# Compact chunks put together with the other order of the first pair, own cross attention banks for odd heads, and 512-column matmuls in the MLP output halves

## The reference

```python
for l in range(DEPTH):
    h = rmsnorm(x, norm_mix[l])
    if l % 2 == 0:
        qkv, z, b_raw, a_raw, lx, lg = split_cols(h @ hyb_in_w[e], HYB_SIZES)
        mix = concat([gdn_mixer(...), rglru_mixer(...)]) @ hyb_out_w[e]
    else:
        mix = swa_mixer(h @ swa_in_w[o], ...) @ swa_out_w[o]
    x = x + mix
    x = x + cross_attn(rmsnorm(x, norm_cross[l]), rmsnorm(mem, norm_mem[l]), ...)
    x = x + conv_ffn(rmsnorm(x, norm_ffn[l]), ...)

def cross_attn(h, mem_n, wq, wkv, wo, q_norm, k_norm):      # 4 heads of 128
    q = rmsnorm((h @ wq).reshape(bsz, s, X_HEADS, X_HD), q_norm)
    k, v = split_cols(mem_n @ wkv, (X_INNER, X_INNER))
    p = softmax(einsum(q, rmsnorm(k, k_norm)) * X_HD ** -0.5)
    return einsum(p, v) @ wo

def conv_ffn(h, w_in, conv_w, conv_b, w_out):
    gt, up = split_cols(h @ w_in, (D_FF, D_FF))
    gt = causal_dwconv(gt, conv_w) + conv_b
    return (silu(gt) * up) @ w_out
```

## Time and profile before

| | |
|---|---|
| median of 3 runs | 2650.51 us (2649.71 to 2658.74) |
| profiled execution | 2661.51 us, its span 2659.7 us |
| PE busy | 2578.9 us, 97% of the span |
| DVE, ACT busy | 1740.7 us (65%), 1138.4 us (43%) |
| mean granted PE clock | 0.991 of full speed |
| weights read | 800 pieces of 512 KB, 162 GB/s over the span |

### The profile page before, as it was taken

How to read it: one execution, slowest core, us unless ns; L and a number is a source line. 1 busy time by engine, 2 the same in 40 slices (tenths; PEclk the granted TensorE clock), 3 DMA queues, 4 the chain that set the end, 5 groups by cost and what they waited for, 6 DMA issues and landing times.

```text
span 2659.7 us, 47742 instructions
## 1 busy us (share of the span) xinstructions
PE 2578.9 (97%) x18995; PEld 2382.9 (90%) x18995; DVE 1740.7 (65%) x2469; ACT 1138.4 (43%) x1501; POOL 50.2 (2%) x58
## 2 busy tenths in 40 slices
PE   7999999998999999999999999999999999999999
PEld 6889888998988899889989888898888998899889
DVE  6566666666777756775577667766777557764773
ACT  5444443443444434443344445444444334443443
POOL 2000000000000000000000100000000000000000
PEclk9999999999999999999999999999999999999999
DMA  6434444355456565656555543354465655665554
GB/s 201 121 112 131 117 120 135 124 180 165 143 166 189 184 187 175 183 189 192 184 184 182 154 146 109 104 161 141 127 189 184 187 173 185 189 193 183 185 185 149
DMA packets 428452, 432.56 MB, mean 163 GB/s; under 512 B 13802, under 2 KB 425747, under 8 KB 428304
## 3 DMA queue, kind: packets, MB, share of 16 engines
q1 hardware_dynamic: 423776, 422.46, 51.7%
q0 software_dynamic: 2304, 5.85, 0.7%
q10 hardware_dynamic: 2224, 2.11, 0.2%
HBM read 428.27 MB, written 2.10 MB: 162 GB/s over the span
## 4 chain that ended last, share of the span: by engine, by line
PE 86%; DVE 7%; ACT 4%; issue 2%; DMA 1%; POOL 0%; POOLq 0%; SPq 0%; ACTq 0%; DVEq 0%
PE stream L1655 25%; PE stream L1640 14%; PE stream L1641 13%; PE stream L1642 13%; PE stream L1656 13%; ACT scores L920 1%; DVE w_lo L986 1%; PE bank L1624 1%; PE bank L1758 1%; ACT w_hi L550 1%; DMA stage<-in_mem 1%; PE bank L1687 0%; DVE v_buf L1040 0%; DVE k_buf L1040 0%; DVE lru_x L1040 0%
## 5 line engine op out<-in xcount | busy, mean ns | idle before, releaser
L986 DVE TENSOR_TENSOR w_lo<-w_raw,w_hi 128x1024 fp32r<-128x1024 f32 x800 | 964.4, 1222 | 553.0 <-ACT w_hi L550 550.0
L550 ACT CAST w_hi<-w_raw 128x1024 fp32r<-128x1024 f32 x800 | 836.3, 1048 | 827.2 <-PE stream L1642 474.4
L1655 PE MATMUL stream<-h,w_hi 128*128 128x512 f32 x2816 | 995.6, 399 | 0.0
L1656 PE MATMUL stream<-h,w_lo 128*128 128x256 f32 x2816 | 790.9, 281 | 0.0
L1655 PEld LDWEIGHTS stream<-h,w_hi 128*128 128x128 f32 x2816 | 529.2, 188 | 131.8
L1640 PE MATMUL stream<-act,w_hi 128*128 128x256 f32 x2016 | 575.4, 285 | 1.0 <-DVE act L1013 1.0
L1642 PE MATMUL stream<-act,w_lo 128*128 128x256 f32 x2016 | 571.4, 283 | 0.0
L1641 PE MATMUL stream<-act,w_hi 128*128 128x256 f32 x2016 | 571.4, 283 | 0.0
L1656 PEld LDWEIGHTS stream<-h,w_lo 128*128 128x128 f32 x2816 | 532.0, 189 | 0.1
L1640 PE MATMUL stream<-h,w_hi 128*128 128x256 f32 x1536 | 460.2, 300 | 5.3 <-DVE w_lo L986 5.3
L1641 PE MATMUL stream<-h,w_hi 128*128 128x256 f32 x1536 | 438.7, 286 | 0.0
(11 more groups left out here) (397 smaller groups left out, 1612.3 us busy)
## 6 DMA issues: line engine op xcount, KB each, us to landing
w_raw<-in_ffn_in_w SPq DMA_DIRECT2D x352, 512.0 KB, 4.5
w_raw<-in_ffn_out_w SPq DMA_DIRECT2D x176, 512.0 KB, 4.6
w_raw<-in_hyb_in_w SPq DMA_DIRECT2D x96, 512.0 KB, 3.8
w_raw<-in_swa_in_w SPq DMA_DIRECT2D x48, 512.0 KB, 3.6
w_raw<-in_xkv_w SPq DMA_DIRECT2D x32, 512.0 KB, 3.4
w_raw<-in_hyb_out_w SPq DMA_DIRECT2D x32, 512.0 KB, 4.2
w_raw<-in_swa_out_w SPq DMA_DIRECT2D x32, 512.0 KB, 3.5
w_raw<-in_xq_w SPq DMA_DIRECT2D x16, 512.0 KB, 4.0
```

The source lines that it names most:

```text
L550: nc.scalar.copy(whi[:, k], raw[:, n % NRAW]).then_inc(hi_split, 1)
L986: v.tensor_tensor(wlo[:, k], raw[:, n % NRAW], whi[:, k].bitcast(F32), ALU.subtract).then_inc(lo_split, 1)
L1655: mm(bank[:, m, :], whi[:, k, kk, w], h[:, kt, :, :], start=(q == 0 and kk == 0), stop=False, skip_group_check=True)
L1656: last = mm(bank[:, m, 0:TOK], wlo[:, k, kk, w], h[:, kt, 0, :], start=False, stop=(q == 3 and kk == len(kts) - 1), skip_group_check=True)
```

## The change

Four edits in one.

1. The output halves of the MLP call `wide_piece` with `act_` as the source instead of `piece`: per pair of blocks one matmul of 512 columns and one of 256, in place of three of 256. DVE's residual of these groups is now two additions, right halves first, then left halves.
2. In cross attention of layer 1, `turn` and `pv` of the odd heads have banks of their own (`B[3]` and `B[0]`), head 1 is turned and copied right behind head 0, and the first two pieces of the product with `xo_w` are cut in two (`xo_heads`): heads 0 and 1 as soon as they are out, heads 2 and 3 at the end. DVE's `norm(2)` stands ahead of `outp(1)`.
3. Ahead of pair 0, x is turned into four banks instead of two; ACT's rounding of a weight piece stands ahead of the x work of its quarter from quarter 1 on; POOL's parameter DMAs wait for the second quarter of x.
4. In pair 0, DVE copies `ba` at the head of tick 3 instead of its end, and the polynomial chain and what follows it (`gates` 6, 7, 8) stand at ticks 8, 9, 10.

```diff
@@ x_bank, x_turned, x_pv
+        def x_bank(g):
+            return B[(1, 2, 4, 5)[g % 4]]
+        def x_turned(layer, h):
+            return B[3] if layer and h % 2 else B[4]
+        def x_pv(layer, h):
+            return B[0 if layer and h % 2 else 5][:, 0:TOK]
@@ gpsimd
+            pool.wait_ge(x_loaded[1], 16)
             pool.dma_start(wba[:], ...)
@@ scalar
             for q in range(4):
+                if q:
+                    split(q)
                 x_hi(2 * q)
                 x_hi(2 * q + 1)
-                split(q)
+                if q == 0:
+                    split(q)
...
-                if t == 7:
+                if t == 9:
                     tables(LN_EXP)
                     act.wait_ge(cols_in, 1)
...
                     if layer and t == 7:
                         copy(0)
+                        copy(1)
...
                     scale(1)
-                    copy(1)
                     exps(2)
                     exps(3)
@@ vector
-                if t == 3:
-                    dve.wait_ge(ba_done, 1)
-                    v.tensor_copy(ba_rows, B[5][0:16, 0:TOK]).then_inc(ba_copied, 1)
...
-                if t == 6:
+                if t == 8:
                     dve.wait_ge(ln_out, 3)
...
                     if p == 0 and t == 3:
+                        dve.wait_ge(ba_done, 1)
+                        v.tensor_copy(ba_rows, B[5][0:16, 0:TOK]).then_inc(ba_copied, 1)
                         dve.wait_ge(ss_done, 1)
...
-                        residual(g0 + g, g, n + g * q + q - 1, "norm_mix" if norm else None, KT, wide(g0 + g)[:, 1, :])
+                        dve.wait_ge(pieces_done, n + g * q + q)
+                        x2, both = xT[:, 2 * g:2 * g + 2, :], wide(g0 + g)
+                        link(v.tensor_tensor(x2, both[:, :, TOK:512], x2, ALU.add))
+                        v.tensor_tensor(x2, both[:, :, 0:TOK], x2, ALU.add).then_inc(group_evac, 1)
+                        if norm:
+                            dve.wait_ge(group_evac, g0 + g + 1)
+                            split_h(g, x2.rearrange("p k c -> p (k c)"), "norm_mix", KT)
...
                     outp(0)
+                    norm(2)
                     outp(1)
-                    norm(2)
                     norm(3)
@@ tensor
-                    if q:
-                        pe.wait_ge(xt_copied, g - 1)
+                    if q >= 2:
+                        pe.wait_ge(xt_copied, g - 3)
...
-                if t == 7:
+                if t == 9:
                     pe.wait_ge(g_ready, 1)
...
+            def xo_heads(g, heads):
+                n, gi = XO[1] + g, GROUP[XO[1]] + g
+                k = n % NSPLIT
+                pe.wait_ge(xo_out, 4 + heads[-1] + 1)
+                if heads[0] == 0:
+                    pe.wait_ge(lo_split, n + 1)
+                    pe.wait_ge(group_evac, gi - 1)
+                for m in range(2):
+                    for kt in heads:
+                        o = ST[gi % 2][:, m * TOK:m * TOK + TOK]
...
+                if heads[-1] == 3:
+                    last.then_inc(pieces_done, 1)
...
                     if layer and t == 7:
                         turn(0)
+                        turn(1)
...
                     scores(3)
-                    turn(1)
                     pv(0)
                     pv(1)
                     turn(2)
+                    turn(3)
+                    xo_heads(0, (0, 1))
                     pv(2)
-                    turn(3)
+                    xo_heads(1, (0, 1))
                     pv(3)
-                pe.wait_ge(xo_out, 4 * layer + 4)
                 for g in range(8):
-                    piece(XO[layer] + g, GROUP[XO[layer]] + g, 0, 0, act_, range(4))
+                    if layer and g < 2:
+                        xo_heads(g, (2, 3))
+                    else:
...
-                            piece(n + g * q_ + q, g0 + g, q, q_ - 1, act_, range(4 * q, 4 * q + 4), wide(g0 + g)[:, 1, :])
+                            wide_piece(n + g * q_ + q, g0 + g, q, range(4 * q, 4 * q + 4), 0, act_, q_ - 1)
```

More of the change, by code:

```diff
@@ L788, in copy @@
                         act.wait_ge(xo_done, 4 * layer + h - 1)
-                    nc.scalar.copy(xpT[:, h % 2], B[4][:]).then_inc(xpt_copied, 1)
+                    nc.scalar.copy(xpT[:, h % 2], x_turned(layer, h)[:]).then_inc(xpt_copied, 1)
                 def scale(j):
@@ L1353, in outp @@
                     dve.wait_ge(xo_done, 4 * layer + h + 1)
-                    split_act(h, B[5][:, 0:TOK], xo_out)
+                    split_act(h, x_pv(layer, h), xo_out)
                 def scale(j):
@@ L1944, in turn @@
                     pe.wait_ge(xpn, 4 * layer + h + 1)
-                    if h:
-                        pe.wait_ge(xpt_copied, 4 * layer + h)
+                    if layer and h >= 2:
+                        pe.wait_ge(xpt_copied, 4 * layer + h - 1)
+                    elif h and not layer:
+                        pe.wait_ge(xpt_copied, h)
                     for u in range(2):
                         for m in range(2):
-                            last = transpose(B[4][:, m * TOK + u * P:m * TOK + u * P + P],
+                            last = transpose(x_turned(layer, h)[:, m * TOK + u * P:m * TOK + u * P + P],
                                              xp[:, h % 2, u * TOK + m * P:u * TOK + m * P + P])
@@ L1954, in pv @@
                     pe.wait_ge(xpt_copied, 4 * layer + h + 1)
-                    if h:
-                        pe.wait_ge(xo_out, 4 * layer + h)
+                    if layer and h == 1:
+                        pe.wait_ge(n_out, N_XQ[layer] + 2)
+                    elif layer and h >= 2:
+                        pe.wait_ge(xo_out, 4 * layer + h - 1)
+                    elif h:
+                        pe.wait_ge(xo_out, h)
                     for m in range(2):
-                        last = mm(B[5][:, 0:TOK], xv[layer][:, m, h, :], xpT[:, h % 2, m * TOK:m * TOK + TOK],
+                        last = mm(x_pv(layer, h), xv[layer][:, m, h, :], xpT[:, h % 2, m * TOK:m * TOK + TOK],
                                   start=(m == 0), stop=(m == 1))
@@ L1975, in cross @@
                 return scores, turn, pv, sums
+            def xo_heads(g, heads):
[8 more added lines that the diff above has]
+                        o = ST[gi % 2][:, m * TOK:m * TOK + TOK]
+                        w = slice(m * P, m * P + P)
+                        mm(o, whi[:, k, kt, w], act_[:, kt, 0, :], start=(m == 0 and kt == 0), stop=False, skip_group_check=True)
+                        mm(o, whi[:, k, kt, w], act_[:, kt, 1, :], start=False, stop=False, skip_group_check=True)
+                        last = mm(o, wlo[:, k, kt, w], act_[:, kt, 0, :], start=False, stop=(kt == 3), skip_group_check=True)
+                if heads[-1] == 3:
+                    last.then_inc(pieces_done, 1)
             def common(layer):
@@ L2046, in common @@
                     turn(2)
+                    turn(3)
+                    xo_heads(0, (0, 1))
                     pv(2)
-                    turn(3)
+                    xo_heads(1, (0, 1))
                     pv(3)
-                pe.wait_ge(xo_out, 4 * layer + 4)
                 for g in range(8):
-                    piece(XO[layer] + g, GROUP[XO[layer]] + g, 0, 0, act_, range(4))
+                    if layer and g < 2:
+                        xo_heads(g, (2, 3))
+                    else:
+                        if g == 0:
+                            pe.wait_ge(xo_out, 4)
+                        piece(XO[layer] + g, GROUP[XO[layer]] + g, 0, 0, act_, range(4))
                     if layer == 0 and g == 0:
```

14 lines of the change are left out of this document (7 added, 7 removed).

## The result

The changed kernel takes 2610.28 us in the median of 4 runs (2620.4, 2601.94, 2602.92, 2617.63), the kernel before 2654.42 us beside it (2650.51, 2658.74, 2649.71, 2658.33): ratio 0.984, 95% interval 0.9802 to 0.9878. The four executions lie in two groups, two near 2602 us and two near 2619 us, and nothing between.

A forecast was written before the change was run, and what follows sets the result against it. PE, busy 97% of the span, was taken to bound the kernel. MLP -8.7, cross attention -6.5 and start -6.9 gave -22.1 us: 2639.4 profiled, 2628.5 us as median (own range 2623 to 2635, whole range 2620 to 2641).

The forecast's parts named there:

- the MLP term: MLP output halves, both layers: 176 pieces each 0.053 us cheaper, less 0.7 us for a last DVE addition; -8.7 us.
- Start: Before and in pair 0: earlier x and reordered `ba` copy and log1p chain; -6.9 us, bounds -10 and 0.
- x: Start: x's second quarter lands earlier with POOL's parameter DMAs held back; -0.9 us, bounds +0.3 and -1.5.
- gates: Pair 0: moved `ba` copy and log1p chain let the Gram products start 6.6 us earlier; -6.0 us taken.
- Cross attention: Layer 1: earlier head 1 transposes and split output product shorten waits and half clock; -6.5 us, bounds -4 and -8.5.
- no fall of the clock at all: Bound for layer 1's cross attention: the scores also take half as long; -8.5 us.
- DVE's second addition at the end of layer 1: End of layer 1: the added residual addition stands on the path to the output; +0.7 us.
- cost nothing: End of layer 0: the added 0.73 us is hidden, since DVE next waits for a DMA landing at 1506.18.
- (b): MLP output halves gain nothing, 512 columns taking two times 120 ns; -12.7 us in all, 2637.8 us; chance 0.07.
- (c): Waits move rather than go: start gains 0, cross attention -4; -12.7 us in all, 2637.8 us; chance 0.17.
- (d): Both waits and the half clock go wholly: -8.7 - 8.5 - 9 = -26.2 us, 2624.3 us; chance 0.12.
- (e): MLP output groups hold two banks until two additions finish, so PE waits: +65 us, 2716 us; chance 0.02.

## Why the prediction was wrong

**The failed step is the size of the MLP term, -8.7 us.** It took the 353.3 ns of the earlier trace rows as the price of a pair of 512 and 256 columns and carried it to all 176 pieces, and it took the input halves for unchanged because their code is. The pair has two prices, 353.3 and 346.7 ns, kept over a whole uninterrupted run of such pairs, hardware loops and halves included. Before, every output half was narrow. Behind a narrow half the wide one was slow in all 16 places of the profiles of before and of the three kernels with narrow output halves. Only chunk 1, entered from other work, was ever fast: 64 pieces, 3.4 us per layer. Now nothing stands between the halves, and a layer that starts fast stays fast over up to 264 pieces, 14.1 us; in layer 1 only up to the last seven groups, where the output's transposes stand between. The -8.7 holds for both layers slow: in the profile with both slow, layer 1's MLP to the end takes 755.1 us against 759.0 before, 3.9 less where 4.0 was forecast. One layer fast adds about 14, both about 28. The nine executions lie there: four at 2602 to 2607, four at 2617 to 2620, one at 2635. In the one profile of before both chunks 1 happened to be slow (181.08 and 181.09 us), so it showed one price only. The kernel before spreads as well, 2643.80 to 2661.26 us in 11 executions measured together; its two chunks 1 can make 6.8 of these 17.5 us, and the rest was not traced.

**At the slow price the rest of the sum nearly fits.** The profiled 2620.4 us has one layer fast; without its 14.1 us it would be 2634.5 against 2639.4 forecast from the profiled execution of before, and the execution with both slow measured 2635.27. The rest, some 5 us, is in the lines below.

- Start: -7.15 us at mixout, forecast -6.9. x -0.84 (forecast -0.9) and gates -6.21 (-6.0), each measured alone. The second x quarter is turned at 8.67 us where 9.5 to 10.5 was guessed, and still the second piece starts at 17.02, inside the forecast's 16.9 to 17.8. The waits of 1.08 and 1.75 us stand where 1.7 and 1.9 were forecast.
- Cross attention: -8.22 us, forecast -6.5; it is near the bound "no fall of the clock at all", -8.5. The gaps became 0.57, 1.20, 0.94 and 0.98 us instead of 1.01, 1.07, 1.77 and 0.97, and here the clock held. The remaining product starts 41.07 us into the stretch instead of 44.78, 3.7 early and not 2.2; the scores alone give 1.3 of this. In the profile with both layers slow the clock did fall once, for 3.4 us, and the stretch takes 70.80 us (1807.60 to 1878.40): 6.7 less than before, which is the forecast. That was one profile of nine.
- DVE's second addition at the end of layer 1: forecast +0.7. PE's wait ahead of the last four transposes grew from 0.78 to 1.51 us, as forecast. At the end of layer 0 it was to "cost nothing": wrong in its working, right or better in the sum. The waits of the last group grew, and a later one shrank. The changed kernel:

```profile
1481.05 1.10 PE L1694 MATMUL bank<-norm_r,cst 128*128 128x256 f32 x4 [1.08 <-POOL norm_r L529]
...
1489.88 2.03 PE L1698 MATMUL bank<-x_sq,cst 128*128 128x256 f32 x4 [2.17 <-ACT x_sq L578]
```

Before, these two waited 0.33 and 1.45 us. But DVE's wait for the DMA of `sinks` fell from 3.84 to 1.59 us, and PE's wait of 3.86 us at 1515.11 is gone: 1.5 us lost, 3.9 won. With the MLP edit alone it is the same (1.08 and 2.17 us, then 0.24), while the three kernels without it keep 3.35 to 3.49 us. PE was to wait for that DMA anyway, so a delay ahead of it was free; why the later wait shrank by more than the delay is not shown.

**The rivals.** (b) is refuted: the wide output halves gain 1.71 us per 32 pieces even at the slow pace. The rule quoted with it ("TensorE: Matmul & The Clock Gate" in the Trainium skill, Back-to-back issue gap) gives, for an isolated matmul, a gap of 2.5 ns over the columns' time. This trace disagrees, in a stream with new weights for each: here it is 13.3 ns for 256 columns alone, and 13.3 or 16.7 ns in the pair. (c) is refuted by the start's -7.15 us. (d) came true for cross attention alone. (e) did not happen: no PE wait on an evacuation in an output half.

**What stays open.** What decides the pace. Shown is that in every profile it held from where a run of alternating pairs began to the next other matmul as long as the clock stood at 1.00, that it differs between executions of one program, that grouping the matmuls by width removes it, and that one fp32 matmul ahead of each group gives an order of three slow groups and one fast. That points to a position of the stream against something periodic, but no counter in the trace shows that, and it is argued only. Nor is it shown why a long narrow stretch led to slow in 16 of 16 while one narrow matmul turned slow into fast in three of five.

## What to carry to other kernels

Before you carry a spacing from one place of a trace to another, measure it at every place where the same instructions run, and in more than one execution: two values in one profile mean that a change elsewhere can move stretches whose code you don't touch. Where the executions of a kernel fall into groups, divide the distance between the groups by the number of times the repeated pattern runs; here 14 us was 6.7 ns times 2112 pairs. And look at what ends a good state (here the narrow half between two wide ones): taking it out can be worth more than the instructions that it saves.

## What the runs showed of the hardware

- A run of alternating matmuls of 512 and 256 columns goes at 353.3 or at 346.7 ns per pair at the clock 1.00, and keeps the one it began with; four of one width and four of the other give 350.9 ns per pair; 256 columns alone 120.0 ns.
- Behind the start of 64 matmuls of one column, weights loaded for each, the clock stood at 0.50 for 24 to 27 us, at each of four places. At the first of them PE was busy 4.50 of 4.50 us before the fall and 4.00 of 4.00 us behind it.
- In cross attention four gaps of 0.57, 1.20, 0.94 and 0.98 us went without a fall of the clock in the profile of the change. Eight of nine profiles of kernels with this edit had none in the stretch, one had 3.4 us at 0.50. Before, with gaps of 1.01, 1.07, 1.77 and 0.97 us, there were two stretches at 0.50, of 3.4 and 10.2 us.
